# Sums of squares of the output norm taken in two pieces inside the head loop, and the root's table loaded at the loop's end

## The reference, cut to what matters

```python
y_na = neighbourhood_attention(q, k, v, na_rpb[l])            # 4 heads x 64 columns
y_mla = latent_attention(c_q, c_kv, k_rope, ...)              # 8 heads x 64 columns
y_conv = short_conv(x_in, gate_b, gate_c, conv_w[l], conv_b[l])  # 4 groups x 64 columns
mixed = jnp.concatenate([y_na, y_mla, y_conv], axis=-1)
mixed = rms_norm(mixed.reshape(b, t, OUT_GROUPS, HEAD_DIM),
                 out_norm_g[l].reshape(OUT_GROUPS, HEAD_DIM)).reshape(b, t, D_MIX)
x = x + g1 * (mixed @ w_out[l])
h2 = ada_norm(x, norm2_g[l], sh2, sc2)
gt, up = jnp.split(h2 @ w_gu[l], 2, axis=-1)
x = x + g2 * ((jax.nn.silu(gt) * up) @ w_down[l])
```

## Time and profile before

| | |
|---|---|
| time, median of 3 runs | 1552.88 us (1552.79 to 1554.51) |
| the profiled execution | 1556.09 us, its span 1554.4 us |
| TensorE busy | 1423.4 us, 92% of the span |
| VectorE busy | 593.3 us, 38% |
| ScalarE busy | 445.9 us, 29% |
| GpSimd busy | 39.0 us, 3% |
| granted clock of TensorE, mean | 0.99 |

### The profile page before, as it was taken

How to read it: one execution, slowest core, us unless ns; L and a number is a source line. 1 busy time by engine, 2 the same in 40 slices (tenths; PEclk the granted TensorE clock), 3 DMA queues, 4 the chain that set the end, 5 groups by cost and what they waited for, 6 DMA issues and landing times. The chain is left out here.

```text
span 1554.4 us, 19758 instructions
## 1 busy us (share of the span) xinstructions
PE 1423.4 (92%) x7955; PEld 847.7 (55%) x7955; DVE 593.3 (38%) x1029; ACT 445.9 (29%) x578; POOL 39.0 (3%) x79
## 2 busy tenths in 40 slices
PE   7999999999999998898899899899898799799998
PEld 7987798444344433333333333333333788788887
DVE  4985447202120210210220220220121776677765
ACT  4654543211121111111111111111111536444343
POOL 1000030000000000000000000000000202000000
PEclk9999999999999999999999999999999999999999
DMA  8597998999999999999999999999999161245552
GB/s 266 167 307 248 325 330 279 372 427 428 428 429 428 430 428 430 428 429 428 429 428 429 428 429 428 429 428 430 428 429 387 59 190 55 96 148 186 181 191 93
DMA packets 130687, 516.98 MB, mean 333 GB/s; under 512 B 11173, under 2 KB 99086, under 8 KB 106030
## 3 DMA queue, kind: packets, MB, share of 16 engines
q1 hardware_dynamic: 130350, 515.24, 83.8%
q10 hardware_dynamic: 288, 1.05, 0.2%
HBM read 515.22 MB, written 1.05 MB: 332 GB/s over the span
## 5 line engine op out<-in xcount | busy, mean ns | idle before, releaser
L1258 PE MATMUL ps<-ring,xg 128*64 128x512 f32 x1536 | 341.5, 594 | 30.2 <-DMA ring<-in_expert_w_up 30.0
L1355 DVE TENSOR_TENSOR glu<-ps,bupT 128x512 f32<-128x512 f32 x32 | 22.1, 692 | 730.7 <-PE ps L1267 730.7
L1258 PEld LDWEIGHTS ps<-ring,xg 128*64 128x64 f32 x1536 | 108.3, 137 | 259.0 <-issue 195.4
L1292 PE MATMUL ps<-ring,act 128*64 128x512 f32 x768 | 170.1, 595 | 7.5 <-DVE act L1365 7.5
L80 ACT ACTIVATE hrow<-ps 128x1024 f32<-128x1024 f32 x32 | 32.7, 1023 | 434.6 <-PE ps L1258 434.6
L2018 PE MATMUL ps<-h_halves,w_hi 128*128 128x512 f32 x352 | 125.1, 400 | 0.5 <-DVE h_halves L2158 0.5
L1258 PE MATMUL ps<-more,xg 128*64 128x512 f32 x512 | 114.2, 594 | 11.5 <-DMA more<-in_expert_w_up 11.5
L1292 PEld LDWEIGHTS ps<-ring,act 128*64 128x64 f32 x768 | 53.7, 137 | 117.1 <-issue 106.0
L2113 DVE TENSOR_TENSOR w_lo<-ring,w_hi 128x2048 fp32r<-128x2048 f32 x37 | 84.8, 2292 | 65.1 <-ACT w_hi L80 65.1
L80 ACT ACTIVATE y<-ps 64x512 f32<-64x512 f32 x64 | 37.8, 591 | 241.7 <-PE ps L1292 241.3
L2020 PE MATMUL ps<-h_halves,w_lo 128*128 128x256 f32 x352 | 99.0, 281 | 0.0
(11 more groups left out here) (407 smaller groups left out, 2115.1 us busy)
## 6 DMA issues: line engine op xcount, KB each, us to landing
ring<-in_expert_w_up SPq DMA_DIRECT2D x96, 2048.0 KB, 31.1
ring<-in_expert_w_down SPq DMA_DIRECT2D x48, 2048.0 KB, 35.3
more<-in_expert_w_up SPq DMA_DIRECT2D x32, 2048.0 KB, 31.5
more<-in_expert_w_down SPq DMA_DIRECT2D x16, 2048.0 KB, 35.3
ring<-in_w_in SPq DMA_DIRECT2D x30, 1024.0 KB, 8.3
ring<-in_w_ada SPq DMA_DIRECT2D x24, 1024.0 KB, 5.8
ring<-in_w_gu SPq DMA_DIRECT2D x22, 1024.0 KB, 5.1
ring<-in_w_down SPq DMA_DIRECT2D x11, 1024.0 KB, 4.9
```

The costliest lines, as they stand in the source:

```text
L1258: last = nc.tensor.matmul(up[a2 * CAP:(a2 + 1) * CAP, u, :], k.xg[:, q, h * CAP:(h + 1) * CAP], w[:, c:c + 512], start=(q == 0), stop=(q = ...
L1292: last = nc.tensor.matmul(down[a2 * CAP:(a2 + 1) * CAP, :], k.act[:, m % 4, m // 4, :], w[:, c:c + 512], start=(m == 0), stop=(m == KF - 1 ...
L1355: link(nc.vector.tensor_tensor(k.glu[:, :, :, :], g, b[:, 0].to_broadcast(wide), ALU.add))
```

## The change

VectorE takes the sums of heads 0 to 3 in step 5 and of heads 4 to 7 in step 9, each behind that step's output, instead of all eight in step 10. ScalarE makes its trial root, and so loads the root's table, at the end of its list in `second_mix` instead of at the start of `output`.

```diff
@@ second_mix, ScalarE
             copy(heads - 1)
+            act.wait_ge(rms_ready, TT)
+            nc.scalar.activation(k.root[:, :], k.eps[:, :], ACT.Sqrt)
@@ second_mix, VectorE
                 if i >= 1:
                     out(i - 1)
+                if i == 5:
+                    dve.wait_ge(o_out, 4)
+                    mix_sums(nc, k, link, 0, 4)
+                if i == 9:
+                    dve.wait_ge(o_out, 8)
+                    mix_sums(nc, k, link, 4, 8)
                 if i == 10:
-                    dve.wait_ge(o_out, 8)
                     dve.wait_ge(cv_out, 1)
                     mix_sums(nc, k, link, 12, 16)
-                    mix_sums(nc, k, link, 0, 8)
             out(heads - 1)
@@ output, ScalarE
             link = chain(k, act, "act")
-            link(nc.scalar.activation(k.root[:, :], k.eps[:, :], ACT.Sqrt))
             act.wait_ge(k.sums, 5)
             nc.scalar.activation(k.sroot[:, 0:32], k.ss[:, 0:32], ACT.Sqrt, ...).then_inc(k.roots, 1)
```

## The result

The changed kernel took 1558.48 us (median of 11 runs, 1553.34 to 1562.97), the kernel before 1553.53 us in the same comparison (11 runs, 1552.67 to 1556.22): ratio 1.0025, 95% interval 1.0016 to 1.0035, so slower by 3.9 us (2.5 to 5.4; the two medians alone lie 4.95 us apart). The two intervals share 1.0016 to 1.0023. I had forecast 1554.1 us and "no change"; the likeliest case failed, and the rival of TensorE's clock is what happened.

A forecast was written before the change was run, and what follows sets the result against it. Head loop bound by TensorE, from head 11 by VectorE's chain; output stage starts serially on VectorE. Terms 1.02 + 1.38 - 1.14 + 0 = +1.26 us on the median 1552.88 gave 1554.1 us, "no change"; range 1551.5 to 1556.6.

The forecast's parts named there:

- the likeliest case: Heads' end and output stage: both moved sums delay, +1.3 us, 1554.1 us, counted as no change; chance 0.62.
- the rival of TensorE's clock: Wait before head 11's transposes grows from 0.99 to 2.37 us, clock falls: +3.74 us in all, 1556.6; chance 0.14.
- Sums in step 5, +1.02 us: VectorE's 1.38 us queued before head 7's maximum: 0.87 remain after a 0.51 us cushion, plus 0.15 for resuming.
- Sums in step 9, +1.38 us: VectorE's sums queued between head 8's output and head 11's maximum, already late, no cushion: +1.38 us.
- End of the heads, -1.14 us: After step 10 VectorE is free when the last values are ready: loop ends at 1322.70 instead of 1323.84.
- The table, 0: ScalarE's root table load, moved behind its last copy, is hidden by 0.23 us under head 11's output: cost 0.
- The sum, +1.26 us: Heads' end to output stage: 1.02 + 1.38 - 1.14 + 0 = +1.26 us, output stage starting about 1.3 us later.
- twice as long, +2.48: At the low clock, head 11's transposes (0.49 us) and sixteen value products (1.99 us) take twice as long: +2.48 us.
- the rival's sum of 3.74: Clock rival's total at head 11: +3.74 us including +2.48 for slow work, 1556.6 us, 0.24% slower; chance 0.14.

The follow-up runs named there:

- The two intervals: 95% intervals of the unedited changed kernel against the kernel before: first measurement 1.0016 to 1.0035, second measurement 1.0005 to 1.0023.
- both trios in front of the wait: Changed kernel with sums of heads 0 to 3 and 4 to 7 between maximum and VectorE's wait for TensorE's values: ratio 0.9995, again 0.9997.
- the kernel where the clock is kept up: Changed kernel plus 20 idle TensorE transposes of the identity in front of head 11's transposes: ratio 0.9999 against the kernel before.
- all three profiles with the long wait: Changed kernel, ratio 1.0025; the same unedited again, 1.0014; changed kernel with sums of heads 0 to 3 back in step 10, 1.0009.
- the repeat: The changed kernel measured once more without an edit, against the kernel before: ratio 1.0014 (1.0005 to 1.0023).
- the second profile of the kernel before: One more profile of the kernel before, unedited: 17.68 us from head 5's transposes to VectorE's first output-stage instruction; no ratio given.

## Why the prediction was wrong

- *Sums in step 5, +1.02 us*: right. Head 7's transposes start 1311.41 - 1308.35 = 3.06 us after head 6's instead of 2.20, so 0.86 late, and reach the next scores after 1.43 us instead of 1.28: 1.01. The profile writes the wait as 0.70, not the 0.9 that I named; the end of the products in front, from which it counts, is modelled.
- *Sums in step 9, +1.38 us*: right (wait 2.37 from 0.99).
- *End of the heads, -1.14 us*: right, and to be had alone: both trios in front of the wait give just this.
- *The table, 0*: right (0.06 gained alone; hidden by 0.21 us with the clock kept up). The drain that the Trainium skill's page "ScalarE: Activation LUTs" adds to a load in "What ACT_TABLE_LOAD costs" does not show here either: the load starts 0.02 us behind the copy and the trial root 1.29 us behind the load's start.
- *The sum, +1.26 us*: measured at 18.94 - 17.68 = 1.26, in the kernel where the clock is kept up.
- *The clock*: here it failed. The step, as the prediction put it, is "Against it: work in front of this gap is dense", and with it the chance of 0.14. Dense work in front did not protect the clock: it fell in all three profiles with the long wait. I had compared the gap of 2.37 us with one row of a short gap without a fall (0.99) and one of a longer gap with a fall (2.7), and called it between the two. The trace of the kernel before had more to say of that longer gap. Its wait in TensorE's list, and the granted clock (0.75) of one microsecond within it:

```profile
269.07 0.58 PE L1231 MATMUL ps<-ident,gate 128*32 128x128 f32 x2 [2.67 <-PEq L863]
...
267.00:268.00 1.00, 0.00 (x0) 0.00 (x0) 0.96 (x8) 0.00 (x0) 0.00 (x0) 0.75 0.42 180
```

The wait began at 269.07 - 2.67 = 266.40, and the mean of 0.75 puts the fall at about 267.5, 1.1 us into it. A wait of 2.37 us is longer than that. The work in front of that wait was light, but the row still stood on the side of the fall, and 0.14 was too little for it. And a single profile in which the clock stays up shows that it can, not that it does. The Trainium skill's page "TensorE: Matmul & The Clock Gate", in the section "HAM oscillation — how this bites in real kernels", has waits between bursts of matmuls take the clock down; the waits of its example are longer than this one, and here 2.37 us in dense work was enough, in three profiles of three.
- *The size of the fall*: "twice as long, +2.48" was too much. The work took 1.94 us longer (0.42 + 1.52), so the rival's sum of 3.74 should read 3.20, and 3.19 was measured.
- *The rest of the number*: the median of before was 1553.53 in the comparison, 0.65 above the 1552.88 of three runs on which I had built. With 3.19 that makes 1556.7 us; the measured median lies 1.8 us above, the repeat 0.6 below its own such sum (1553.48 + 3.19 against 1556.05). By the ratio the first comparison has 3.9 us (2.5 to 5.4), which holds the 3.19. So of the 4.4 us between forecast and median, 0.65 are the start, 1.93 the clock, and the cause of the other 1.8 stays open; the scatter of the runs would be enough for it.
- *The cover*: I also gave no price to the cover that VectorE's lateness had been for TensorE: I counted the end of the late sums as a gain of 1.14 us, and not as 0.8 us of protection lost.

## What to carry to other kernels

Work that is put into an in-order queue delays what stands behind it, and the idle time that it may use is the one behind its place: in front of a wait a trio of 1.38 us was free, one place later it cost 1.01 and 1.38 us. Price a longer wait of TensorE not only by itself but by what the work that follows takes at the lower clock, from rows at that clock where there are any, and don't take one profile with the clock up as proof that the wait is harmless. An engine that is late on its own account hides delays of the others; whoever takes its lateness away should look at what it had covered.

## What the runs showed of the hardware

- Behind waits of 2.37 us in dense work the granted clock fell 0.8 us before TensorE went on in two profiles and 1.1 us after it in one. With this wait filled it stayed up, in one profile.
- In three of eight profiles it fell behind a wait of only 0.99 or 1.00 us, when TensorE had gone on for 1.5 to 2.0 us (in the second profile of the kernel before, at 1319.8, with the work resumed at 1317.72). 64 waits of about this length earlier in the same kernel had no fall.
- Sixteen products of 128x64 took 1.99 us at the upper clock and 3.51 at the lower, a factor of 1.76 and not 2; thirty transposes of 128x128 took 5.38 us, mostly at the lower one, and 3.47 at the upper.
- A table load, with the copy before it and the root after it, followed on without a gap: 1322.76 + 0.60 to 1323.38, and 1.29 us to 1324.67.
